# Matrix products of a two-stack network: moving columns taken in pieces of 32 or 64, and xT, daT and yT moved by 64 or 256 bytes

## What is computed

```
x = x + 0.5 * _swiglu(_rmsnorm(x, ffn1_norm[i]), ffn1_w_gate[i], ffn1_w_up[i], ffn1_w_down[i])
proj = _rmsnorm(x, mix_norm[i]) @ w_in[i]                       # first stack, 3600 columns
...
x = x + jnp.concatenate([o_dn, o_hy], axis=-1) @ w_out[i]
...
proj = einsum('bsd,de->bse', rmsnorm(x, norm_mix_g[l]), w_in[l])  # second stack, 6400 columns
y = gate0 * (o_da @ w_branch_da[l]) + gate1 * (o_ret @ w_branch_ret[l]) + gate2 * (o_sc @ w_branch_sc[l])
x = x + einsum('bsd,de->bse', y, w_out[l])
gu = einsum('bsd,df->bsf', rmsnorm(x, norm_ffn_g[l]), w_ffn_in[l])
x = x + einsum('bsf,fd->bsd', silu(conv(g)) * u, w_ffn_out[l])
```

## Time and profile before

| | |
|---|---|
| median of 3 runs | 2014.07 us (2013.45 to 2014.14) |
| profiled execution, its own time | 2016.84 us |
| profiled execution, span of the trace | 2014.9 us |
| PE busy | 1978.3 us (98%), 15795 matmuls |
| PE weight loads busy | 1820.1 us (90%) |
| GpSimd busy | 1493.5 us (74%) |
| ScalarE busy | 1038.7 us (52%) |
| VectorE busy | 945.3 us (47%) |
| moved by DMA | 329.10 MB, 163 GB/s |

### The profile page before, as it was taken

How to read it: one execution, slowest core, us unless ns; L and a number is a source line. 1 busy time by engine, 2 the same in 40 slices (tenths; PEclk the granted TensorE clock), 3 DMA queues, 4 the chain that set the end, 5 groups by cost and what they waited for, 6 DMA issues and landing times.

```text
span 2014.9 us, 37053 instructions
## 1 busy us (share of the span) xinstructions
PE 1978.3 (98%) x15795; PEld 1820.1 (90%) x15795; DVE 945.3 (47%) x1589; ACT 1038.7 (52%) x1551; POOL 1493.5 (74%) x652
## 2 busy tenths in 40 slices
PE   7999999999999999999999999999999999999998
PEld 7998788989989998788899989999999899999997
DVE  3550766434205550776343304745576028356750
ACT  5444456464436444456464547455644374656442
POOL 6789454459887789446368887768789977687896
PEclk9999999999999999999999999999999999999999
DMA  6756332136555656333135565545555655455553
GB/s 222 243 178 209 105 126 92 41 123 197 186 202 176 217 184 204 94 105 106 44 127 189 188 236 160 168 147 183 173 178 197 198 159 163 147 193 170 179 200 126
DMA packets 250965, 329.10 MB, mean 163 GB/s; under 512 B 9008, under 2 KB 225586, under 8 KB 250418
## 3 DMA queue, kind: packets, MB, share of 16 engines
q1 hardware_dynamic: 250802, 326.73, 49.6%
HBM read 325.66 MB, written 1.05 MB: 162 GB/s over the span
## 4 chain that ended last, share of the span: by engine, by line
PE 60%; DVE 3%; issue 1%; ACT 1%; POOL 0%; DVEq 0%; ACTq 0%
PE psA L410 12%; PE psA L411 12%; PE psA L412 12%; PE psB L410 5%; PE psB L412 5%; PE psB L411 5%; PE psB L1939 1%; PE psA L1781 1%; DVE hT_lo L1168 1%; PE psA L2111 0%; PE psA L2113 0%; PE psA L1782 0%; PE psA L1787 0%; DVE small L1522 0%; PE psB L2101 0%
## 5 line engine op out<-in xcount | busy, mean ns | idle before, releaser
L1022 POOL TENSOR_TENSOR w_lo<-raw,w_hi 128x1024 fp32r<-128x1024 f32 x600 | 1457.9, 2448 | 501.0 <-ACT w_hi L597 500.1
L410 PE MATMUL psA<-xT_hi,w_lo 128*128 128x256 f32 x3168 | 897.5, 283 | 6.2 <-POOL w_lo L1022 4.1
L411 PE MATMUL psA<-xT_lo,w_hi 128*128 128x256 f32 x3168 | 884.7, 279 | 0.0
L412 PE MATMUL psA<-xT_hi,w_hi 128*128 128x256 f32 x3168 | 883.8, 279 | 0.0
L597 ACT ACTIVATE w_hi<-raw 128x1024 fp32r<-128x1024 f32 x600 | 630.4, 1052 | 362.7 <-PE psB L412 237.5
L410 PEld LDWEIGHTS psA<-xT_hi,w_lo 128*128 128x128 f32 x3168 | 594.9, 188 | 17.5 <-issue 11.8
L411 PEld LDWEIGHTS psA<-xT_lo,w_hi 128*128 128x128 f32 x3168 | 594.4, 188 | 3.4 <-issue 3.3
L412 PEld LDWEIGHTS psA<-xT_hi,w_hi 128*128 128x128 f32 x3168 | 594.0, 187 | 0.0
L1168 DVE TENSOR_TENSOR hT_lo<-hfull,hT_hi 128x256 fp32r<-128x256 f32 x132 | 219.9, 1698 | 2.1 <-ACT hT_hi L730 0.8
L410 PE MATMUL psB<-w_hi,hT_lo 128*128 128x512 f32 x528 | 205.6, 389 | 0.4 <-issue 0.4
L412 PE MATMUL psB<-w_hi,hT_hi 128*128 128x512 f32 x528 | 205.5, 389 | 0.0
(11 more groups left out here) (440 smaller groups left out, 2303.8 us busy)
## 6 DMA issues: line engine op xcount, KB each, us to landing
raw<-in_w_in SPq DMA_DIRECT2D x78, 1024.0 KB, 5.1
raw<-in_ffn_w_gate SPq DMA_DIRECT2D x44, 1024.0 KB, 5.2
raw<-in_ffn_w_up SPq DMA_DIRECT2D x44, 1024.0 KB, 5.2
raw<-in_ffn_w_down SPq DMA_DIRECT2D x44, 1024.0 KB, 4.9
raw<-in_w_ffn_in SPq DMA_DIRECT2D x44, 1024.0 KB, 4.9
raw<-in_w_ffn_out SPq DMA_DIRECT2D x22, 1024.0 KB, 4.8
raw<-in_w_out SPq DMA_DIRECT2D x16, 1024.0 KB, 4.8
raw<-in_w_branch_da SPq DMA_DIRECT2D x4, 1024.0 KB, 4.9
```

The source lines that it names most:

```text
L410: nc.tensor.matmul(o, a_lo, b_hi, start=start, stop=False, skip_group_check=skip)
L411: nc.tensor.matmul(o, a_hi, b_lo, start=False, stop=False, skip_group_check=skip)
L412: return nc.tensor.matmul(o, a_hi, b_hi, start=False, stop=stop, skip_group_check=skip)
L1022: nc.gpsimd.tensor_tensor(split_half(w_lo, n, kind), raw_half(n, kind), split_half(w_hi, n, kind).bitcast(F32), ALU.subtract)\
```

## The change

Every product with xT as moving operand, and `project_two`, now takes its moving columns in another order: in pieces of 32, first piece 0, then piece 4, 1, 5, 2, 6, 3, 7. The output columns are written in the same order, so each value still goes to its own place. For 256 columns of xT the two pieces of a pair are 512 bytes apart, and a piece is 128 bytes. The unused tile ahead of xT grows from 16 to 32 words, so xT begins 128 bytes past a multiple of 512 and not 64. The first branch (daT) takes pieces of 64 in the same way, `into_x` of yT (512 moving columns of weights) also takes pieces of 64, and daT and yT begin 256 bytes past a multiple of 512. `into_x` of hT is as before, and so is that of xT in its order of columns, though xT has a new place. The number of instructions, their order on every engine and all waits are the same.

```diff
-        sb("line", [P, 16])
+        sb("lines", [P, 32])
...
-        daT_hi = at("daT_hi", 60, [P, 4, L], F32R)
-        daT_lo = at("daT_lo", 64, [P, 4, L], F32R)
-        yT_hi = at("yT_hi", 60, [P, KC, L], F32R)
-        yT_lo = at("yT_lo", 68, [P, KC, L], F32R)
+        daT_hi = at("daT_hi", 60.25, [P, 4, L], F32R)
+        daT_lo = at("daT_lo", 64.25, [P, 4, L], F32R)
+        yT_hi = at("yT_hi", 60.25, [P, KC, L], F32R)
+        yT_lo = at("yT_lo", 68.25, [P, KC, L], F32R)
...
+        def step(v, piece=32):
+
+            if len(v.shape) == 3:
+                return v.rearrange("p h (j n) -> p j h n", n=piece)
+            return v.rearrange("p (h j n) -> p j h n", h=2, n=piece)
+
+        def product(o, a_hi, a_lo, b_hi, b_lo, start, stop, skip=False, piece=0):
+
+            if piece:
+                o, b_hi, b_lo = step(o, piece), step(b_hi, piece), step(b_lo, piece)
...
-                    ins_ = product(o, hi[:, kc, :], lo[:, kc, :], xT_hi[:, kc, :], xT_lo[:, kc, :], kc == 0, kc == KC - 1)
+                    ins_ = product(o, hi[:, kc, :], lo[:, kc, :], xT_hi[:, kc, :], xT_lo[:, kc, :], kc == 0, kc == KC - 1,
+                                   piece=32)
...
-                        M(psA[:, t, 0:L], split_half(w_hi, s + t, "A")[:, kc, :], xT_hi[:, kc, :], start=False, stop=False)
+                        M(step(psA[:, t, 0:L]), split_half(w_hi, s + t, "A")[:, kc, :], step(xT_hi[:, kc, :]), start=False, stop=False)
...
                         ins_ = product(o[:, rb * L:(rb + 1) * L], xT_hi[:, kc, t], xT_lo[:, kc, t], hi[:, :, kc, :], lo[:, :, kc, :],
-                                       kc == 0, kc == KC - 1)
+                                       kc == 0, kc == KC - 1, piece=32)
...
-                            ins_ = product(psB[:, 2 * rb + c, :], a_hi[:, k, t], a_lo[:, k, t], hi[:, v], lo[:, v], starts, ends)
+                            ins_ = product(psB[:, 2 * rb + c, :], a_hi[:, k, t], a_lo[:, k, t], hi[:, v], lo[:, v], starts, ends, piece=64 if st and made is s2["yb_lo"] else 0)
...
                                 ins_ = product(o, hi[:, v], lo[:, v], x_hi[:, k, :], x_lo[:, k, :], i == 0 and c % 2 == 0,
-                                               i == n - 1, skip=True)
+                                               i == n - 1, skip=True, piece=64 if r == 0 else 32)
```

More of the change, by code:

```diff
@@ L406, in split_half @@
             return v.rearrange("p (c n) -> p c n", c=KC) if kind == "A" else v
-        def product(o, a_hi, a_lo, b_hi, b_lo, start, stop, skip=False):
+        def step(v, piece=32):
[5 more added lines that the diff above has]
+                o, b_hi, b_lo = step(o, piece), step(b_hi, piece), step(b_lo, piece)
             nc.tensor.matmul(o, a_lo, b_hi, start=start, stop=False, skip_group_check=skip)
@@ L1780, in project_entry @@
                     for t in range(2):
-                        M(psA[:, t, 0:L], split_half(w_lo, s + t, "A")[:, kc, :], xT_hi[:, kc, :], start=(kc == 0), stop=False)
-                        M(psA[:, t, 0:L], split_half(w_hi, s + t, "A")[:, kc, :], xT_hi[:, kc, :], start=False, stop=False)
+                        M(step(psA[:, t, 0:L]), split_half(w_lo, s + t, "A")[:, kc, :], step(xT_hi[:, kc, :]), start=(kc == 0), stop=False)
+                        M(step(psA[:, t, 0:L]), split_half(w_hi, s + t, "A")[:, kc, :], step(xT_hi[:, kc, :]), start=False, stop=False)
                 for kc in range(KC):
@@ L1786, in project_entry @@
                     for t in range(2):
-                        ins_ = M(psA[:, t, 0:L], split_half(w_hi, s + t, "A")[:, kc, :], xT_lo[:, kc, :], start=False, stop=(kc == KC - 1))
+                        ins_ = M(step(psA[:, t, 0:L]), split_half(w_hi, s + t, "A")[:, kc, :], step(xT_lo[:, kc, :]),
+                                 start=False, stop=(kc == KC - 1))
                         if kc == KC - 1:
@@ L2245, in last_branch @@
                             ins_ = product(psA[:, b, (c % 2) * L:(c % 2 + 1) * L], hi[:, v], lo[:, v], xT_hi[:, k + i, :],
-                                           xT_lo[:, k + i, :], i == 0 and c % 2 == 0, i == 1, skip=True)
+                                           xT_lo[:, k + i, :], i == 0 and c % 2 == 0, i == 1, skip=True, piece=32)
                         if m == 3:
```

## The result

The changed kernel takes 2037.31 us (median of 4 runs, 2036.92 to 2037.86) against 2014.11 us before (4 runs): a ratio of 1.0114, 95% interval 1.0102 to 1.0126. It is slower by 23 us. The forecast was 1971 us, the range ended at 2020, and slower had a chance of 0.14.

The account below looks back on a forecast made before the run. PE's pace through its matmuls was taken to bound the kernel. Gains of 41.4 us (xT products and project_two) and 1.3 us (daT) sum to 42.7 us, taking the median from 2014.07 to 1971.4 us; range 1955 to 2020.

Parts of the forecast that it names:

- What bounds the kernel: Whole kernel: PE's pace through its matmuls ends it, PE busy 98% of the span at 2.4 GHz.
- Three levels in the trace: 256-column products: 113.3, 117.8 and 120.0 ns, read as moving columns and next weights meeting in the same part of memory.
- Without a meeting I take the 113.3 ns: Products moving xT and project_two: 9,313 starts go from 117.8 to 113.3 ns, gaining 41.4 us.
- the worst end of that very term: Products moving xT and project_two: all at daT's 120.0 ns, a loss of 25.5 us.
- The order in pieces costs nothing: Products in pieces: project_two's two runs at 113.2 ns put a read jump under 0.2 ns; written jumps were unseen.
- The rival's 0.58 ns: Price per jump, seven jumps in each product, at which the 41.4 us gain is used up.
- daT, yT and into_x of xT: Other products: daT gains 1.3 us or 0, yT 0, xT as loaded operand 0 (gain 1 to loss 0.8 us).
- The rival that came true: Products in pieces: each jump in stream or output has a price; smaller gain, 1988 to 2009 us, 0.14; slower 0.14.
- The second rival: PE chains: level set by pipelines falling into step at chain start, not addresses; nothing changes, 2010 to 2018 us, chance 0.10.

Follow-up runs that it names:

- The probe: Network left out, PE alone, 40 series of 72 products over places and column orders; plain order at 0, 64, 128, 192 bytes: 119.5, 117.8, 118.5, 114.2 ns.
- the second probe: Network left out, PE alone, 38 series reading pieces chosen distances apart; with 16 weight columns, 32 to 160 apart: 113.8, 117.9, 113.5, 117.9, 113.8 ns.
- the probes: Three programs without the network, PE alone: places and orders, distances between pieces, and runs behind different breaks; the last gave both levels at 64 and 192.

## Why the prediction was wrong

**What bounds the kernel: right.** PE ends it, at full clock, through the length of its products and nothing else. The profiled executions of the seven kernels follow the sum of distances of the products with xT. Sum and span are 1238.4 and 2014.9 us before, 1250.0 and 2025.7 with pieces alone, 1253.4 and 2029.2 with places alone, 1259.4 and 2035.1 with both, 1223.6 and 2000.1 with xT at 192, 1230.5 and 2004.8 with daT there too, 1249.9 and 2025.4 for the change at 192. Set against the kernel before, the change of the sum and that of the span agree within 2.2 us each time.

**Three levels in the trace: right, and read one step too far.** 113.3, 117.8 and 120.0 ns are there. The step that failed is "Without a meeting I take the 113.3 ns". It rests on two claims that no row carried, that the change keeps the streams apart and that its order costs nothing. The first I took from the change's own numbers, a period of 512 bytes or less, and for a period of 256 the 128 bytes were as unproven as any other. The probe says that the period is 256, and that in plain order 128 is worse (118.5) than the 64 of before (117.8). The term was +41.4 us of gain; measured, the sum of distances grew by 21.0 us, with 9,829 of 10,272 products at 120 ns. That is close to the loss of 25.5 us that I had as the worst end of that very term. By that end the time is 2014 + 25 = 2039 us, and the range as given ended at 2020: the bound was worked out and then not used. That it fits so well is luck: 120.0 was daT's in plain order at 0, and here it is what pieces of 32 and the place 128 make together. Nor was 113.3 tied to weights that are out of the way: `project_two`, with 128 weight columns, had it in about half of its products, and by the records the load of 16 columns takes 94 ns and that of 128 takes 188, half as long and not an eighth.

**The order in pieces costs nothing: wrong.** This is the second claim. I had 0 from project_two, whose moving columns come in two runs 4096 bytes apart at 113.2 ns. That row shows a jump from half 1 of one period to half 0 of another, and such a jump is free, as the second probe confirms. It doesn't speak for 0, 4, 1, 5, where every second step stays in the same half. The price is 4.4 ns for seven such steps (four are made by the change, and cost 3.5 ns with 16 weight columns). It works out to 0.6 to 0.9 ns a step in the probes. The rival's 0.58 ns was for each of seven jumps, 4.1 ns a product. By its own sum 3.5 ns would have left 5 us of the gain; the kernel became slower because there was no gain to use up, and the place took more.

**daT, yT and into_x of xT: right in size.** daT was given 1.3 us or 0 and got 0, yT 0 and got 0: for them the change moves by a whole period and swaps stretches that are alike. xT as loaded operand went from 394 to a median of 393.

**The rival that came true** is the first, in part. Its mark was named in advance, a minimum over 276 in gate_columns too, and that is what the trace shows. But it put the price on the jump, and of the place it said only that two streams in step on the same part would show over 120 ns. In plain order at 128 bytes the distances stay under that on average, at 119.1 ns (those up to 125 counted), and yet this place costs 14 us by itself. Its chance of 0.14 was too low: the trace of before had two unlike values for two places (117.8 at 64, 120.0 at 0) and a low level that came and went at one of them, so the levels were not explained by places, and a forecast of 113.3 for all needed them to be.

**The second rival, that the level is set by how two pipelines fall into step**, had the better account of 113.3 and 117.8, both of which come at 64 and at 192. It was wrong in that it made places count for nothing: they set how often the low level comes (6 of 55 runs at 64, 30 of 56 at 192), and at 0 and 128 with 128 weight columns no run of the probes in plain order came to it.

**Two rules set against measurements.** The Trainium skill's page "TensorE: Matmul & The Clock Gate", section "Step-by-step: what each phase is for", says the weight load takes no read bandwidth from the running matmul. The probes don't agree: with 128 weight columns places give 114 to 120 ns, and at 0 bytes 32 weight columns give 113.7 where 128 give 119.5. The Trainium skill's page "PSUM — Partial Sum Buffer", section "Specifications (TRN2)", says that any non-contiguous pattern slows matmuls significantly. Output in pieces of 32 words costs nothing here, 117.8 against 117.8 at 64, so for pieces of that size the measurement decides against it.

## What to carry to other kernels

Where PE bounds, take the distance of starts by form and look for levels, and before a layout is changed for them, measure the levels by themselves: 40 combinations of place and order fit in one launch of 457 us, and a table of them would have spared this change. Repeat each entry behind different breaks, since one run can land on either of two levels. And take the place from what moves to what is loaded, as the two change roles within one kernel. A level that comes and goes at the same addresses is not explained by addresses; a forecast may not give the best of the levels to all products. Here plain order with xT at 192 bytes and not 64 past the weights is 0.6% faster than the kernel before, and half of its products still run at the upper level.

## What the runs showed that I had not expected

- The place of the moving operand against the loaded one counts modulo 256 bytes for float32r products of 256 columns and 128 weight columns: 119.5, 117.8, 118.5 and 114.2 ns at 0, 64, 128 and 192, and steps of 32 bytes make a difference too. Why 192 is best, and 128 isn't, is open.
- Reading 128 bytes twice in a row from the same half of a 256-byte period costs 0.6 to 0.9 ns, with 16 weight columns loaded.
- A stream keeps one of two speeds, 113.3 or 117.8 ns, through hundreds of products (862 in a row in one block of the kernel with xT at 192) until something breaks it. That this makes the time of one program spread is likely but not shown, each kernel having one trace: four runs of that kernel lie between 2000.26 and 2005.75 us, and seven of the kernel before between 2013.04 and 2018.98.
- What is left of 113.3 over the 106.7 ns of 256 columns at 2.4 GHz was there in every plain case, with 16 or 32 weight columns too, and nothing tried here took it away.
